# A two-layer fp32 decoder trunk on one core: who makes the stored sum of three weight tiles in the first unit of each layer

## The reference

```python
# layer A: w_in is 2048 x 12288
h = rms_norm(x, norm_g)
u, v, z = jnp.split(h @ w_in, 3, axis=-1)
...
# layer B: w_in is 2048 x 8208
h = rms_norm(x, norm_g)
proj = h @ w_in
q, k, v, z, f_logit = jnp.split(proj, [...], axis=-1)
```

## Time and profile before

| | us |
|---|---|
| time of three runs | 2215.6, 2217.64, 2220.31 (median 2217.64) |
| the profiled execution's own time | 2216.75 |
| its span in the trace | 2215.0 |
| TensorE busy in the span | 2199.7 (99%) |
| VectorE busy | 1761.6 (80%) |
| ScalarE busy | 1185.0 (53%) |
| GpSimd busy | 282.0 (13%) |

### The profile page before, as it was taken

One profiled execution on the slowest core, in us unless ns is written; L12 is line 12 of the kernel. 1 busy time (PEld: TensorE's weight loads), 2 busy tenths in 40 slices (PEclk: granted clock), 3 DMA queues, 4 the chain that ended last, 5 costly groups with the idle time before them and its releaser, 6 DMA issues.

```text
span 2215.0 us, 27231 instructions
## 1 busy us (share of the span) xinstructions
PE 2199.7 (99%) x10150; PEld 1821.8 (82%) x10150; DVE 1761.6 (80%) x2152; ACT 1185.0 (53%) x1702; POOL 282.0 (13%) x381
## 2 busy tenths in 40 slices
PE   8999999999999999999999999999999999999999
PEld 6888888888888888888878888888888888888887
DVE  8978878877877877889798488977987888677666
ACT  6856645554554554666455555554565455443432
POOL 0011001001211211211200000110210210221100
PEclk9999999999999999999999999999999999999999
DMA  7788877879888988999997865686786797874333
GB/s 272 258 273 272 257 254 247 251 253 280 271 271 263 285 263 251 332 318 309 343 335 233 288 193 182 205 270 210 217 292 215 220 299 252 262 246 165 116 105 124
DMA packets 270772, 551.12 MB, mean 249 GB/s; under 512 B 22896, under 2 KB 48080, under 8 KB 269616
## 3 DMA queue, kind: packets, MB, share of 16 engines
q1 hardware_dynamic: 206240, 396.95, 56.2%
q0 software_dynamic: 37808, 104.16, 15.8%
q10 hardware_dynamic: 26592, 48.27, 5.7%
HBM read 449.60 MB, written 120.78 MB: 258 GB/s over the span
## 4 chain that ended last, share of the span: by engine, by line
PE 93%; DVE 4%; DMA 1%; issue 1%; ACT 0%; SPq 0%; ACTq 0%; DVEq 0%
PE ps L1517 16%; PE ps L1524 16%; PE ps L1520 14%; PE ps L1491 9%; PE ps L1501 9%; PE ps L1496 9%; PE ps L1956 2%; PE ps L1954 2%; PE ps L1955 2%; PE ps L1854 2%; PE ps L1529 2%; PE ps L1800 1%; PE ps L1679 1%; PE ps L1727 1%; PE ps L1729 1%; PE ps L1728 1%
## 5 line engine op out<-in xcount | busy, mean ns | idle before, releaser
L968 ACT ACTIVATE u_hi<-raw 128x1024 fp32r<-128x1024 f32 x368 | 389.6, 1059 | 496.7 <-PE ps L1524 303.0
L2030 DVE TENSOR_TENSOR u_lo<-raw,u_hi 128x1024 fp32r<-128x1024 f32 x368 | 449.1, 1220 | 213.7 <-ACT u_hi L968 213.1
L975 ACT ACTIVATE u_hi<-raw 128x512 fp32r<-128x512 f32 (+1 forms) x368 | 311.3, 846 | 205.6 <-PE ps L1524 102.4
L2037 DVE TENSOR_TENSOR u_lo<-raw,u_hi 128x512 fp32r<-128x512 f32 (+1 forms) x368 | 350.1, 951 | 18.1 <-ACT u_hi L975 17.4
L1517 PE MATMUL ps<-u_hi,x1h 128*128 128x512 f32 x1056 | 282.9, 390 | 0.0
L1524 PE MATMUL ps<-u_lo,x1h 128*128 128x512 f32 x1056 | 282.4, 389 | 0.0
L1520 PE MATMUL ps<-u_hi,x1l 128*128 128x512 f32 x960 | 256.6, 389 | 0.0
L2005 DVE TENSOR_TENSOR raw<-raw 128x1024 f32<-128x1024 f32 x184 | 224.0, 1217 | 19.0 <-DMA raw<-in_b_w_in_dram 12.7
L1524 PEld LDWEIGHTS ps<-u_lo,x1h 128*128 128x128 f32 x1056 | 198.2, 188 | 41.6 <-DVE u_lo L2030 0.4
L1517 PEld LDWEIGHTS ps<-u_hi,x1h 128*128 128x128 f32 x1056 | 197.7, 188 | 40.6
L1520 PEld LDWEIGHTS ps<-u_hi,x1l 128*128 128x128 f32 x960 | 180.2, 188 | 37.4
(11 more groups left out here) (271 smaller groups left out, 3477.5 us busy)
## 6 DMA issues: line engine op xcount, KB each, us to landing
raw<-in_a_w_in_dram SPq DMA_DIRECT2D x280, 512.0 KB, 4.8
raw<-in_b_w_in_dram SPq DMA_DIRECT2D x184, 512.0 KB, 4.8
t_rows<-t ACTq DMA_DIRECT2D x184, 256.0 KB, 5.8
raw<-t_rows SPq DMA_DIRECT2D x184, 256.0 KB, 5.4
raw<-in_a_w_out_dram SPq DMA_DIRECT2D x72, 512.0 KB, 7.0
w_raw<-in_b_w_out_dram SPq DMA_DIRECT2D x64, 256.0 KB, 2.8
yf_rows<-y POOLq DMA_DIRECT2D x16, 512.0 KB, 5.1
yf_rows<-yf_rows POOLq DMA_DIRECT2D x64, 128.0 KB, 5.6
```

The lines of the kernel that those rows point to most:

```text
L968: act.activation(first_tiles(hi), first_tiles(m), ACT.Copy).then_inc(hi1_first, 1)
L975: act.activation(other_tiles(hi, u, ph), other_tiles(m, u, ph), ACT.Copy).then_inc(hi1_ready, 1)
L2030: dve.tensor_tensor(first_tiles(lo), first_tiles(m), first_tiles(hi), ALU.subtract)\
L2037: dve.tensor_tensor(other_tiles(lo, u, ph), other_tiles(m, u, ph), other_tiles(hi, u, ph), ALU.subtract).then_inc(lo1_ready, 1)
```

## The change

In the first unit of each layer (16 steps) VectorE no longer runs `sum_t2`. ScalarE stores place 0 of the raw slot, the sum of two tiles, directly to `t2_dram`. Then GpSimd issues a DMA that reads the third tile from the weights in DRAM and adds it to the rows stored (`accum_op`). SyncE loads the rows in half 1 only after this adding DMA (`t2_added`, which reuses semaphores of later stages, whose counts move by 32). Because the store now reads the raw slot itself, SyncE also waits for the store before it loads a slot again that a step of half 0 of a first unit had used (`t2_source`). The other units keep `sum_t2`. The function `weights` is moved without a change.

```diff
+        t2_added = cum_loaded + qkT_loaded + vz_loaded
+
+        def t2_sums(u):
+
+            return KP * (u - (u > 0) - (u > UB))
+
+        def t2_source(g):
+
+            for u in (0, UB):
+                if g is not None and step_of(u, 0, 0) <= g < step_of(u, 1, 0):
+                    return u * KP + g - step_of(u, 0, 0)
+
...
+                stored = t2_source(user_of[g])
+                if stored is not None:
+                    sp.wait_ge(t2_stored[stored % 2], (stored // 2 + 1) * 16)
...
                 else:
                     q = u * KP + k
                     sp.dma_start(slot[:, 1:4:2, :], k2).then_inc(loaded, 16)
-                    sp.wait_ge(t2_stored[q % 2], (q // 2 + 1) * 16)
+                    if first(u):
+                        sp.wait_ge(t2_added[k], 32 if u else 16)
+                    else:
+                        sp.wait_ge(t2_stored[q % 2], (q // 2 + 1) * 16)
                     sp.dma_start(slot[:, 2, :], t2_dram[k, :, :]).then_inc(loaded, 16)
 
...
+            def add_t2(u, k):
+
+                q = u * KP + k
+                pool.wait_ge(t2_stored[q % 2], (q // 2 + 1) * 16)
+                pool.dma_start(t2_dram[k, :, :], weights(u, 2 * k * P)[:, 1, :], accum_op=ALU.add).then_inc(t2_added[k], 16)
+
+            for k in range(KP):
+                add_t2(0, k)
             pool.wait_ge(means_ready, 2)
             power(rstd_a[:, :], msx_a[:, 1, :], NT).then_inc(rstda_ready, 1)
 
...
+            for k in range(KP):
+                add_t2(UB, k)
             pool.wait_ge(means_ready, 6)
             power(rstd[:, :, 0], msx[:, 1, :], NT).then_inc(rstd_ready, 1)
...
             def store_t2(u, k):
                 q = u * KP + k
-                act.wait_ge(t2_ready, q + 1)
+                if first(u):
+                    g = step_of(u, 0, k)
+                    act.wait_ge(t_ready, g + 1)
+                    if q >= 2:
+                        act.wait_ge(t2_stored[q % 2], q // 2 * 16)
+                    act.dma_start(t2_dram[k, :, :], raw_of(g)[:, 0, :]).then_inc(t2_stored[q % 2], 16)
+                    return
+                act.wait_ge(t2_ready, t2_sums(u) + k + 1)
                 act.dma_start(t2_dram[k, :, :], t2[:, q % 2, :]).then_inc(t2_stored[q % 2], 16)
...
-                    pe.wait_ge(qkT_loaded[h % HG], 16 * (h // HG + 1))
+                    pe.wait_ge(qkT_loaded[h % HG], 32 + 16 * (h // HG + 1))
...
@@ -2214,13 +2249,11 @@
                 if k == 0:
                     low_first(0, 0, 0)
                     x_low1(0)
-                    sum_t2(0, 0)
                     low_other(0, 0, 0)
                     dve.wait_ge(rows_T, 2)
                     dve.tensor_copy(cols[:, KC:3 * KC], pY[:, 0, 0:2 * KC]).then_inc(cols_ready, 1)
                     sums(0, 0, 1)
                 else:
-                    sum_t2(0, k)
                     if k + 1 < KP:
...
                             sums(UB, 0, 0)
-                            sum_t2(UB, 0)
                         elif k == 14:
```

More of the change, by code:

```diff
@@ L510, in y_of, with weights @@
             return y_s[:, s, :, :] if s < 3 else y_s3[:, :, :]
+        def weights(u, row):
+            if u < VU:
+                return a_v[row:row + P, u, :, :]
+            if is_out(u):
+                c = (u - NU) % 2 * 2 * FB
+                row += (u - NU) // 2 * 2 * KP * P
+                return a_out[row:row + P, c:c + 2 * FB].rearrange("r (s c) -> r s c", s=2)
+            if u < NU:
+                return a_uz[row:row + P, :, (u - VU) * FB:(u - VU + 1) * FB]
+            g0, g1 = HALVES[u - UB]
+            c = (0 if KIND[u - UB] == "qk" else 2 * D) + g0 * FB
+            apart = D + (g1 - g0) * FB
+            o = max(0, c + 2 * apart - 4 * D)
+            return b_w_in[0][row:row + P, c - o:c - o + 2 * apart].rearrange("r (s c) -> r s c", s=2)[:, :, o:o + FB]
+        t2_added = cum_loaded + qkT_loaded + vz_loaded
[5 more added lines that the diff above has]
+                    return u * KP + g - step_of(u, 0, 0)
         @block.sync
@@ L521, in load_x @@
                 sp.dma_start(stage[:, n % 3, :, :], x_t[:, :, c * 2 * P:(c + 1) * 2 * P]).then_inc(x_loaded[n % 3], 16)
[L523 to L536, removed]
             def load_step(u, ph, k):
@@ L837, in mask_cum @@
             def mask_cum(h):
-                pool.wait_ge(cum_loaded[h % 2], 16 * (h // 2 + 1))
+                pool.wait_ge(cum_loaded[h % 2], 32 + 16 * (h // 2 + 1))
                 for b0, b1 in ((5, 8), (1, 2)):
@@ L1846, in attend @@
                 p, e = h // 2, h % 2
-                pe.wait_ge(vz_loaded[p % 2], 32 * (p // 2 + 1))
+                pe.wait_ge(vz_loaded[p % 2], 32 + 32 * (p // 2 + 1))
                 pe.wait_ge(probsT_ready, h + 1)
@@ L2353, in _ @@
                 if k == 1:
-                    sum_t2(UB, 1)
                     low(UB, 0, 1)
@@ L2366, in _ @@
                     x_low1b(2 * KP - 7 + k)
-                if k + 1 < KP:
-                    sum_t2(UB, k + 1)
-                else:
+                if k + 1 == KP:
                     x_sums2b(2 * KP - 2)
```

## The result

Median of six runs 2231.38 us (2230.93 to 2233.69) against 2219.53 us for the kernel before (six runs, 2215.60 to 2221.92). The ratio is 1.0057, 95% interval 1.0047 to 1.0067, so +12.6 us (+10.4 to +14.9); the two medians lie 11.9 us apart. The forecast was 2217.5 us, its range 2214.2 to 2223.0. In what follows, differences from the kernel before are this ratio less 1, times 2218 us, with the interval in brackets; profiled executions scatter by 2 us and more and only show where time goes. Two slow executions, one of 10586 us of the kernel before and one of 7633 us of an experiment (e18), are left out of the ratios.

The account below looks back on a forecast made before the run. TensorE, busy 99% of the span, was taken as the bound. Layer A -0.9 + 0.5 and layer B +0.25 gave -0.15 us: profiled 2216.75 to 2216.6, predicted median 2217.5 us, range 2214.2 to 2223.0.

Parts of the forecast that it names:

- Part 1: First units: sixteen sums leave VectorE, removing TensorE's waits for it; 0.9 us gained in layer A, up to 0.90 in B.
- Layer A's held slot: Layer A, step 4: load issued at 18.1, landing at 24.1 against a limit of 24.6; cost 0, at most 2.0 us.
- Part 2: First units: slots held until the store lands delay loads; cost 0 in layer A, +0.25 us in layer B.
- Layer B's load of step 6: Layer B: issued at 1319.0, landing at 1325.2 (1324.0 to 1327.5); +0.25 us, bounds -0.90 and +2.55.
- The engine time of an addition: Each 256 KB adding DMA was taken to occupy all 16 DMA engines for 1.5 us, with 2.17 as the bound.
- Part 3: Layer A: three adding DMAs delay the load of step 6 to 34.1 against 34.6; charged 0.5 us, bounds 0 and 4.3.
- Part 4: Half-1 loads' wait for additions, GpSimd's list and ScalarE's wait for stores cost nothing; cover over 10 us for the loads.
- rival 2: Both layers: held slots and adding DMAs make the four-slot ring the bound; +5.95 us, 2223.6, perhaps 2 more; chance 0.20.
- Both signs that the prediction named for being wrong: TensorE standing still over 2 us in either first unit, or an adding DMA landing in over 12 us.
- the signs of the late loads: Step 4's second load issued near 18 us, VectorE waits of 1 us or more in B, DMA share above 0.8 at 32-44 us.

Follow-up runs that it names:

- e18: Kernel before plus 16 adding DMAs beside the first units into an unread DRAM tensor, each issued only after the previous landed: +2.9 us (+0.9 to +4.9).
- e11: Kernel before with 12 of VectorE's 16 sums cut to one column, no adding DMAs, no held slots: -2.4 us (-4.4 to -0.4).
- e1: Kernel before with slots held until the store of the three-tile sum has landed, no adding DMAs: +1.1 us (-1.1 to +3.1) against before.
- e5: The change in layer A's first unit alone, layer B as before: +3.3 us (+1.3 to +5.3) against the kernel before.
- e13: Kernel before plus 16 adding DMAs into an unread DRAM tensor, spread one at a time over units after the first: -0.7 us (-2.7 to +1.3).
- e7: Changed kernel with additions into an unread DRAM tensor, half-1 loads waiting only for the store: +12.4 us (+9.5 to +15.1) against before.
- e10: Kernel before plus 16 adding DMAs into an unread DRAM tensor, eight in a row behind each layer's first unit: +9.5 us (+6.7 to +12.2).
- e4: Changed kernel with its 16 adding DMAs turned into plain copies of the same tiles: +3.3 us (+1.3 to +5.3) against the kernel before.
- e14: Kernel before plus 16 plain DRAM-to-DRAM copies of the same tiles beside the first units, into an unread tensor: 0.0 us (-2.0 to +2.0).
- e15: Kernel before plus 8 adding DMAs (odd steps of both first units) into an unread DRAM tensor: -0.9 us (-2.9 to +1.1).
- e3: Kernel before plus 16 adding DMAs beside the first units into an unread DRAM tensor, no held slots: +6.0 us (+4.0 to +8.0).
- e12: Kernel before with held slots and 16 adding DMAs into an unread DRAM tensor, VectorE still summing: +11.8 us (+9.1 to +14.6).
- e9: Changed kernel with ScalarE issuing each store ahead of the step's copies: +14.0 us (+10.9 to +17.1) against the kernel before.
- e8: Kernel before with the 16 sums made by GpSimd in SBUF, slots held until it has read them, no adding DMAs: +8.0 us (+5.3 to +10.9).

## Why the prediction was wrong

- **TensorE's waits for VectorE and their worth (Part 1): right.** e11 measures -2.4 us (-4.4 to -0.4) for 12 of the 16 sums, where the prediction had 1.8 for all and 2 at most; the interval holds both. In the changed kernel both waits of layer A at half 1 are gone, but a new one of 0.57 us on ScalarE stands there and the start had moved by 4.4 us.
- **Layer A's held slot (Part 2): right.** Step 4 was in time; e1 costs +1.1 us (-1.1 to +3.1).
- **Layer B's load of step 6 (Part 2), with no term for adding DMAs in layer B (Part 3): the step that failed.** It was to be issued at 1319.0 and to land in 0.4 + 4.6 to 8.1 us, for +0.25, at most +2.55. On that clock the issue was 2.4 us before the forecast (1323.74, less the 7.1 us by which the unit came later), but its second tile took 16.1 us, twice the upper bound, and landed 5.7 us past the latest time forecast (1340.3 less 7.1, against 1327.5): layer B alone is +10.2 us. The three additions beside it held the DMA engines for 5.4 us, and the sum had no term for them. The bound came from a full stretch without additions; there was no row of loads beside them, and I still took "some adding DMAs beside it" as small. Step 5 of layer B had no term either: its load waited for a slower store, went out at 1322.75, 7.1 us later than before on the same clock, and cost TensorE the 1.48 us at 1331.25.
- **The engine time of an addition (Part 3): right in layer A, low in layer B, and charged in one place only.** 1.5 us of all engines was taken; the trace after gives 19.1% of 60 us for eight, 1.43 us, in layer A, and 1.8 us each for the three behind 1323 us in layer B. In layer A step 5 was the late one, by 2.6 us, since its second tile took 12.4 us, above the 8.1 of Part 2; step 6 had been charged with 0.5. The change there is +3.3 us (e5), beside the +4.3 - 0.9 = +3.4 that the upper bound gives. The fit of the Trainium skill (DMA: Bandwidth & Descriptors, the section on the anatomy of one DMA from GpSimd), by which Part 3 has an estimated 2.6 us for such a DMA, doesn't agree with these traces: an addition lands in 6.7 us where it has room (e13) and in 7.4 in layer A.
- **The clock: missing.** No term for it: 1.5 us in A and about 2.5 in B behind the waits, in the profiled execution after.
- **Waits that cost nothing (Part 4): nothing speaks against it for the half-1 loads** (e7). But ScalarE's store was not treated as part of a cycle that the additions slow: rival 2 named it, "a store that is itself slowed", for 2 us more.
- Rival 2 had the mechanism, at 0.20 and half the size (+5.95). Both signs that the prediction named for being wrong came: TensorE stood for 2.52 and 7.07 us, and three additions landed in 13.1 us in the median. So did the signs of the late loads (second load of step 4 at 18.09 us, VectorE's waits of 3.46 and 7.89 us in layer B, a DMA share of 1.06 to 1.08 from 32 to 44 us), which forecast and rival 2 share.

What stays open: why an addition holds the DMA engines twice as long as a copy of the same bytes, and longer still where several are queued (1.43 us each in layer A, 1.8 in the bunch of layer B, an estimated 2.2 in e10's row, from 81.9% of 16 us for 1.59 MB). The runs show that the loss needs the addition (e4, e14) and many of them close together (e13, e15, e18), not what inside the DMA engines or the DRAM does it. About 3 us of the profiled execution after lie between 100 and 1290 us, in short waits at places that e3 and e5 show as well; which late transfer causes them wasn't looked into.

## What to carry to other kernels

Before a sum is moved from a busy engine into an adding DMA, measure its engine time from a trace and add it to the landing of every load that shares the stretch with it. Here the additions showed no cost where they were spread out (16) or halved (8), and where three met three pairs of loads two tiles landed in 16 us instead of 4.6 to 8.1. A wait that chains a load to a store's landing was cheap alone (+1.1 us) and together with the additions cost more than the sum of both: measure the two together. When an idle time of TensorE like those here, of 2.2 us and more, is forecast, add what the lower clock costs behind it (1.5 to 2.5 us here).

## What the hardware showed that I had not expected

- An adding DMA of 256 KB from DRAM to DRAM is 144 packets against 80 for the copy, takes twice the engine time (1.43 to 1.5 us against 0.7 in layer A's first 60 us) and lands in 5.9 to 7.4 us with room (medians, e13, e15), against 5.7 and 6.0 for the copies of e14; eight in a row land in 10.8 us (layer A) and 17.6 (layer B, where the DMA engines have a share of 1.03 at 152 GB/s).
- The loads beside additions keep their engine time per MB (2.8 us against 2.7 before, 24 to 32 us of layer A); the GB/s fall because the additions hold the engines.
- Sixteen plain copies of the same bytes beside the same loads cost 0.0 us (-2.0 to +2.0).
- The granted clock was 1.00 up to the waits in the profile after and 0.54 to 0.62 in the 4 to 8 us behind waits of 2.5 and 7 us; behind the one of 1.48 us in layer B it stayed at 1.00. Other runs agree: 0.64 behind a wait of 2.24 us (e5), 0.58 behind one of 4.32 (e12), 1.00 behind one of 1.96 (e9).
- GpSimd's addition of 128 x 512 elements takes 1.68 us in layer A and lengthens VectorE's subtraction beside it from 1.21 to 2.31 us (e8).
